# A two-block transformer in exact-split fp32: the weight ring goes from two slots of 2048 columns to four of 1024, and VectorE takes over GpSimd's half of one subtraction

## The reference

```
# first block
u = moba_attention(rms_norm(x), w_qkv, w_o)      # 8 heads of 128; 256 tokens are one block: causal softmax with a distance bias
h = x + rms_norm(u)
h = h + rms_norm(squared_relu_mlp(rms_norm(h)))  # square(relu(h @ w_up)) @ w_down, hidden width 4096
# second block, two layers, each with m = silu(c) @ ada_w + ada_b  (1024 -> 6 * 1024)
x = x + g_m * (mixer(modulate(rms_norm(x), sh_m, sc_m)) @ w_out)
x = x + g_f * swiglu(modulate(rms_norm(x), sh_f, sc_f))   # (silu(h @ w_gate) * (h @ w_up)) @ w_down, hidden width 2816
# mixer of layer 0: w_in (1024 -> 2560), short convolution and a gated linear recurrence (LRU)
# mixer of layer 1: w_qkv, norms of q and k, stick-breaking attention with 16 heads of 64
```

## Time and profile before

| what | value |
|---|---|
| three runs | 1019.25, 1021.16, 1027.04 us; median 1021.16 |
| span of the profiled execution, first to last instruction | 1019.1 us (the profile has no other time of it) |
| mean granted TensorE clock, share of full speed | 0.981 |
| weights and modulation weights read | 206.91 MB from HBM, 204 GB/s over the span |

### The profile page before, as it was taken

How to read it: one execution, slowest core, us unless ns; L and a number is a source line. 1 busy time by engine, 2 the same in 40 slices (tenths; PEclk the granted TensorE clock), 3 DMA queues, 4 the chain that set the end, 5 groups by cost and what they waited for, 6 DMA issues and landing times.

```text
span 1019.1 us, 14930 instructions
## 1 busy us (share of the span) xinstructions
PE 935.0 (92%) x5777; PEld 817.1 (80%) x5777; DVE 693.5 (68%) x582; ACT 447.7 (44%) x481; POOL 527.6 (52%) x224
## 2 busy tenths in 40 slices
PE   5989988999998999779999999989889899999997
PEld 4978777888887688758888898867658698988986
DVE  4378489999999679995678787475997643222234
ACT  4434543334434546535333433365666344333431
POOL 5744454454554365645655555534543445555553
PEclk9999989999999999999999999999889999999999
DMA  6546367888887287552788887434322334554552
GB/s 221 175 134 227 96 251 256 292 319 319 317 312 278 76 312 246 187 205 87 275 305 284 293 305 266 165 124 166 123 83 84 123 125 166 185 185 165 172 192 90
DMA packets 116962, 208.59 MB, mean 205 GB/s; under 512 B 7107, under 2 KB 82987, under 8 KB 110774
## 3 DMA queue, kind: packets, MB, share of 16 engines
q1 hardware_dynamic: 115574, 199.54, 56.1%
q10 hardware_dynamic: 1152, 8.39, 2.3%
q0 software_dynamic: 192, 0.05, 0.0%
HBM read 206.91 MB, written 1.05 MB: 204 GB/s over the span
## 4 chain that ended last, share of the span: by engine, by line
PE 30%; issue 21%; DVE 21%; POOL 18%; ACT 6%; DMA 2%; POOLq 1%; SPq 0%; DVEq 0%; ACTq 0%
POOL w_lo L525 17%; DVE mod L1067 6%; DVE w_lo L940 5%; ACT w_hi L646 4%; PE acc L1397 4%; PE acc L1398 4%; PE acc L1399 4%; PE acc L1452 2%; PE acc L1457 2%; PE acc L1454 2%; DVE x L1021 1%; PE ub L1397 1%; PE ub L1399 1%; PE ub L1398 1%; PE acc L1419 1%
## 5 line engine op out<-in xcount | busy, mean ns | idle before, releaser
L525 POOL TENSOR_TENSOR w_lo<-w_raw,w_hi 128x1024 fp32r<-128x1024 f32 x144 | 464.7, 3227 | 408.0 <-ACT w_hi L646 407.9
L646 ACT ACTIVATE w_hi<-w_raw 128x2048 fp32r<-128x2048 f32 (+1 forms) x144 | 274.4, 1906 | 310.2 <-PE ub L1399 111.4
L940 DVE TENSOR_TENSOR w_lo<-w_raw,w_hi 128x1024 fp32r<-128x1024 f32 x144 | 233.6, 1622 | 167.3 <-ACT w_hi L646 167.0
L1397 PE MATMUL ub<-aT_hi,w_hi 128*128 128x256 f32 x896 | 256.0, 286 | 15.2 <-POOL w_lo L525 10.2
L1398 PE MATMUL ub<-aT_lo,w_hi 128*128 128x256 f32 x896 | 253.6, 283 | 0.0
L1399 PE MATMUL ub<-aT_hi,w_lo 128*128 128x256 f32 x896 | 253.5, 283 | 0.0
L1397 PEld LDWEIGHTS ub<-aT_hi,w_hi 128*128 128x128 f32 x896 | 171.8, 192 | 25.7 <-issue 21.9
L1398 PEld LDWEIGHTS ub<-aT_lo,w_hi 128*128 128x128 f32 x896 | 172.0, 192 | 0.0
L1399 PEld LDWEIGHTS ub<-aT_hi,w_lo 128*128 128x128 f32 x896 | 171.9, 192 | 0.0
L1067 DVE SCALAR_TENSOR_TENSOR mod<-ada_raw,silu_c,mod 128x2048 f32<-128x2048 f32 x46 | 171.8, 3736 | 0.1
L1452 PE MATMUL acc<-w_hi,hT_hi 128*128 128x512 f32 x304 | 123.4, 406 | 6.7 <-issue 3.0
(11 more groups left out here) (229 smaller groups left out, 1198.4 us busy)
## 6 DMA issues: line engine op xcount, KB each, us to landing
ada_raw<-in_l_ada_w SPq DMA_DIRECT2D x40, 1024.0 KB, 7.4
w_raw<-in_l_ffn_w_gate SPq DMA_DIRECT2D x44, 512.0 KB, 4.6
w_raw<-in_l_ffn_w_up SPq DMA_DIRECT2D x44, 512.0 KB, 4.5
w_raw<-in_l_ffn_w_down SPq DMA_DIRECT2D x44, 512.0 KB, 3.9
w_raw<-in_w_up SPq DMA_DIRECT2D x32, 512.0 KB, 4.7
w_raw<-in_w_down SPq DMA_DIRECT2D x32, 512.0 KB, 4.3
w_raw<-in_attn_w_qkv SPq DMA_DIRECT2D x24, 512.0 KB, 4.6
w_raw<-in_l_w_qkv SPq DMA_DIRECT2D x24, 512.0 KB, 4.5
```

Of the source, the lines that this page charges most:

```text
L525: pool.tensor_tensor(w_lo[:, s, LO_V:], w_raw[:, s, LO_V:], w_hi[:, s, LO_V:].bitcast(F32), ALU.subtract).then_inc(lo_p_done, 1)
L646: act.activation(w_hi[:, u % 2, c], w_raw[:, u % 2, c], ACT.Copy).then_inc(hi_done, 1)
L940: dve.tensor_tensor(w_lo[:, s, 0:LO_V], w_raw[:, s, 0:LO_V], w_hi[:, s, 0:LO_V].bitcast(F32), ALU.subtract).then_inc(lo_v_done, 1)
L1397: pe.matmul(outp, ah, bh, start=start and k == 0, stop=False)
```

## The change

The ring keeps its bytes and is cut in four slots of 1024 columns, called parts; a unit is two parts in a row. Each part has its own load semaphore, and `hi_done`, `lo_done` and `w_used` now count parts. The transfers are the same (288 of 512 KB). ScalarE makes `w_hi` with two copies of 1024 columns per unit, VectorE makes both rests of a unit, GpSimd none; GpSimd keeps its other work, with nothing queued between. TensorE waits part by part and multiplies part by part: in `project` and `project_T` the loop over parts is now the outer one, in `down` the loop over the two row blocks, and the last of the three matmuls of a block now follows the other two instead of standing behind all of them. The number of matmuls of each shape stays.

```diff
-LO_V = 1024
+PART = UNIT // 2
+SLOTS = 4
...
-        w_raw = sb("w_raw", [P, 2, UNIT])
+        w_raw = sb("w_raw", [P, SLOTS, PART])
...
-            def load_unit(u, pieces, i=None, per=0):
-                if u >= 2:
-                    sp.wait_ge(lo_v_done, plus(u - 1, i, per))
-                    sp.wait_ge(lo_p_done, plus(u - 1, i, per))
-                for dst, src in pieces:
-                    sp.dma_start(dst, src).then_inc(w_loaded[u % 2], 16)
+            def load_part(v, n, src, i, per):
+                if v >= SLOTS:
+                    sp.wait_ge(lo_done, plus(v - SLOTS + 1, i, 2 * per))
+                dst = w_raw[:, v % SLOTS, :].rearrange("p (k n) -> p k n", n=n)
+                sp.dma_start(dst, src).then_inc(w_loaded[v % SLOTS], 16)
...
-            def split_lo(u, i=None, per=0):
-                if u >= U_END:
-                    return
-                pool.wait_ge(hi_done, plus(u + 1, i, per))
...
-                pool.tensor_tensor(w_lo[:, s, LO_V:], w_raw[:, s, LO_V:], w_hi[:, s, LO_V:].bitcast(F32),
-                                   ALU.subtract).then_inc(lo_p_done, 1)
...
-                act.wait_ge(w_loaded[u % 2], plus(32 * (u // 2 + 1), i, 16 * per))
-                if u >= 2:
-                    act.wait_ge(w_used, plus(u - 1, i, per))
-                c = slice(0, LO_V if u == 0 else UNIT)
-                act.activation(w_hi[:, u % 2, c], w_raw[:, u % 2, c], ACT.Copy).then_inc(hi_done, 1)
+                for v in range(2 * u, 2 * u + (1 if u == 0 else 2)):
+                    act.wait_ge(w_loaded[v % SLOTS], plus(16 * (v // SLOTS + 1), i, 16 * 2 * per // SLOTS))
+                    if v >= SLOTS:
+                        act.wait_ge(w_used, plus(v - SLOTS + 1, i, 2 * per))
+                    act.activation(w_hi[:, v % SLOTS, :], w_raw[:, v % SLOTS, :], ACT.Copy).then_inc(hi_done, 1)
...
-                dve.wait_ge(hi_done, plus(u + 1, i, per))
-                s = u % 2
-                dve.tensor_tensor(w_lo[:, s, 0:LO_V], w_raw[:, s, 0:LO_V], w_hi[:, s, 0:LO_V].bitcast(F32),
-                                  ALU.subtract).then_inc(lo_v_done, 1)
+                for v in range(2 * u, 2 * u + 2):
...
+                        dve.wait_ge(hi_done, hi_count(v, i, per))
+                    n = v % SLOTS
+                    dve.tensor_tensor(w_lo[:, n, :], w_raw[:, n, :], w_hi[:, n, :].bitcast(F32),
+                                      ALU.subtract).then_inc(lo_done, 1)
...
-            def unit_ready(u, i=None, per=0):
-                pe.wait_ge(lo_v_done, plus(u + 1, i, per))
-                pe.wait_ge(lo_p_done, plus(u + 1, i, per))
+            def part_ready(v, i=None, per=0):
+                pe.wait_ge(lo_done, plus(v + 1, i, 2 * per))
...
             def project_T(u, h, banks, i=None, per=0):
...
+                for q in range(2):
+                    v = 2 * u + q
+                    part_ready(v, i, per)
+                    for f in range(2):
+                        outp = banks[f][:, h * TOK:(h + 1) * TOK]
+                        for k in range(4):
+                            c, b = slice(k * HALF + f * P, k * HALF + (f + 1) * P), 4 * q + k
+                            wh, wl = w_hi[:, v % SLOTS, c], w_lo[:, v % SLOTS, c]
+                            pe.matmul(outp, wh, aT_hi[:, b, :], start=b == 0, stop=False)
+                            pe.matmul(outp, wh, aT_lo[:, b, :], start=False, stop=False)
+                            last = pe.matmul(outp, wl, aT_hi[:, b, :], start=False, stop=b == KB - 1)
+                    last.then_inc(w_used, 1)
```

More of the change, by code:

```diff
@@ L570, in _ @@
             for step, n in ATT_STEPS:
-                if step == "H" and n < 16:
-                    split_lo(U_QKV1 + n)
-                elif step == "E" and n < 3:
+                if step == "E" and n < 3:
                     start_sums(0, n * UNIT, (n + 1) * UNIT)
[L575 to L584, removed]
+            for _ in range(4):
+                row_rstd()
             pool.wait_ge(xn_done, 12)
@@ L587, in _ @@
             for step, n in LRU_STEPS:
[L588 to L590 removed]
+                if step == "P":
                     pool.wait_ge(lru_u, 2)
@@ new lines, in project_tile @@
+            def project_tile(v, t, k, outp, op_hi, op_lo, start, stop):
+                s, q = v % SLOTS, slice(t * P, (t + 1) * P)
+                for n in range(2):
+                    c = slice(n * CH, (n + 1) * CH)
+                    pe.matmul(outp, op_hi[:, k + n, q], w_hi[:, s, c], start=start and n == 0, stop=False)
+                    pe.matmul(outp, op_hi[:, k + n, q], w_lo[:, s, c], start=False, stop=False)
+                    last = pe.matmul(outp, op_lo[:, k + n, q], w_hi[:, s, c], start=False, stop=stop and n == 1)
+                return last
@@ new lines, in project @@
+                    pe.wait_ge(y_lo, lo_count)
+                    for q in range(2):
+                        for t in range(NT):
+                            for k in range(2 * q, 2 * q + 2):
+                                c = slice((k % 2) * CH, (k % 2 + 1) * CH)
+                                last = pe.matmul(bank(t), op_lo[:, k, t * P:(t + 1) * P], w_hi[:, (2 * u + q) % SLOTS, c],
+                                                 start=False, stop=h != first and k == 3)
+                        last.then_inc(w_used, 1)
@@ new lines, in project @@
+                    return
+                if tile0:
+                    for t in range(NT):
+                        for q in range(2):
+                            if t == 0:
+                                part_ready(2 * u + q, i, per)
+                            last = project_tile(2 * u + q, t, 2 * q, bank(t), op_hi, op_lo, h == first and q == 0,
+                                                h != first and q == 1)
+                            if t == 1:
+                                last.then_inc(w_used, 1)
+                        if t == 0:
+                            last.then_inc(tile0_done, 1)
+                    return
@@ L1422, in project @@
+                for q in range(2):
+                    part_ready(2 * u + q, i, per)
                     for t in range(NT):
-                        for k in range(4):
-                            last = pe.matmul(bank(t), op_lo[:, k, t * P:(t + 1) * P], rhs[k][0], start=False,
-                                             stop=h != first and k == 3)
+                        last = project_tile(2 * u + q, t, 2 * q, bank(t), op_hi, op_lo, h == first and q == 0,
+                                            h != first and q == 1)
@@ new lines, in down_block @@
+            def down_block(v, k, t, n, start, stop, lo=True):
+                s, q, c = v % SLOTS, slice(t * P, (t + 1) * P), slice(n * CH, (n + 1) * CH)
+                outp = acc[:, 2 * t + n, :]
+                pe.matmul(outp, hT_hi[:, k, q], w_hi[:, s, c], start=start, stop=False)
+                last = pe.matmul(outp, hT_hi[:, k, q], w_lo[:, s, c], start=False, stop=False)
+                if lo:
+                    last = pe.matmul(outp, hT_lo[:, k, q], w_hi[:, s, c], start=False, stop=stop)
+                return last
```

248 lines of the change are left out of this document (114 added, 134 removed).

## The result

The changed kernel takes 953.08 us (median of four runs, 952.81 to 953.43) against 1023.51 (four runs, 1019.25 to 1027.04): a ratio of 0.9319, 95% interval 0.929 to 0.9348.

A forecast was written before the change was run, and what follows sets the result against it. TensorE, busy 935.0 of 1019.1 us, was taken as the main bound, with weight-making setting the end over a good quarter of the span. 1019.1 − 27 − 8 − 13 + 3 = 974, plus 2 for the median: 976 us, range 957 to 1001.

The forecast's parts named there:

- GpSimd's hold: VectorE stands still, marked as busy, while GpSimd subtracts: 56 us excess in the rests, 64 us in the sums.
- Rival D: VectorE's long lengths are its own, so it becomes the bound in MLP and LRU: slower, 1052 us; chance 0.04.
- Rival C: Loads become the bound; MLP and first SwiGLU loops keep their periods, losing 6 + 8 us of gain: 990 us; chance 0.06.
- Rival B: Only MLP and SwiGLU loops gain, 16 + 6 us; attention, LRU and stick-breaking stages do not: 999 us; chance 0.14.
- First term: TensorE's waits for weight rests, 33.5 us in 43 waits, go except a fifth, for units behind norms: −27 us.
- Second term: TensorE's restarts around 43 waits for rests, 0.24 us each beyond the wait's length, four fifths saved: −8 us.
- Third term: Chains GpSimd lengthens without naming a rest (`hT_lo`, first `down` unit, residual additions, three more places): −13 us, sure to half.
- costs: The second rest stands ahead of the norms' work at about three stage ends, 1.1 us each: +3 us.

## Why the prediction was right in kind and too small in size

**The mechanism was right.** VectorE's long lengths were GpSimd's hold: the subtractions that nobody uses bring them back, and memsets don't. And where GpSimd makes every second rest again, the waits that come back name VectorE's rest. Rival D is out with it: VectorE needs 18.59 us of a 22.42 us slice. Rival C is out: both loops run without idle time at 0.91 of the transfer engines. Rival B is out for attention and the LRU, which gave 26 us; in the stick-breaking stage its number holds, with 1.5, but what is late there was not shown: with GpSimd's last subtractions on VectorE TensorE's idle time there grew.

**First term, too small.** Waits that name a rest fell from 33.5 to 0.6 us, −32.9 where I let a fifth stay and took −27. The units behind a norm, for which I kept it, no longer wait for a rest. One wait has only changed its name: at the second half of the LRU's output product TensorE waited 1.6 us for GpSimd's rest and now waits 3.1 for the operand `aT_hi`.

**Second term, the step that failed.** "43 x 0.24 = 10 us, of which four fifths: −8 us" stands for all that TensorE's busy time would lose; it lost 22.8. The price of a restart was right: the second SwiGLU with two of the inserted waits grew by 7.1 us, of which 5.2 idle and some 1.5 low clock, which leaves 0.2 for each restart. What it counted was wrong. It has only the waits that name a rest: all named waits went from 78.2 us in 71 to 33.1 in 27, so 44 restarts went and not 34. And the clock was left out altogether: by windows of 1 us TensorE was granted half speed for 37.6 us before and 20.5 after, the idle end of the program not counted. The two traces tell the parts, if from each of the 5777 matmuls to the start of the next the busy time is set against the median of its shape: 11.9 of the 22.8 us lie in matmuls beside a named wait (0.27 for each of 44), 8.6 in matmuls at the low clock (101 before, 53 after), and 2.3 in all the others. Boundaries without an idle entry, like the one at 252.9, can thus be no more than a small part. The low clock was to be seen in the profile before: in the page's mean of 0.981 and in the 0.96 of the LRU stretch.

**Third term and costs.** Idle time that names no rest fell by 45.3 − 32.9 = 12.4 us, against 13 less 3 of costs. (The five items listed add up to 12.3 and not 13.) That the size fits is in part luck, for the time came only in part from the places listed. The wait for `hT_lo` went, and so did the 3.0 us before the first `down` unit. But the waits for a norm's result fell only from 14.1 to 13.3 in sum, with nothing at the second QKV (1.2 and 1.2), while those for the modulation, which the list does not have, fell from 7.5 to 3.0. The residual additions are at 1285 and 692 ns in the mean, as their short twins foretold, `hT_lo` at 1219 in place of 2868. Of the costs one place shows: in the LRU stage unit 12's two rests (392.21 to 394.56) stand on VectorE ahead of the product for which TensorE waits the 3.1 us. ScalarE's 20 us more of busy time show as no wait of their own.

In sum: 32.9 + 12.4 + 22.8 = 68.1. The low end of the range had the three terms whole and 8 us of unnamed idle time, but restarts for 43 waits alone and no clock.

## What to carry to other kernels

When an instruction shows two lengths for one shape, look at what the other engines do at its start before pricing more of it: here work moved onto the engine that looked saturated made that engine less busy. Two remedies for one wait are not added: each freed the loops alone. And price a wait as its length, the restart, and, where the windows show one behind it, the stretch at 1.2 GHz. In these runs every wait of 3 to 6 us behind the first matmuls had one, and of those of 2.0 to 2.3 us some had one and some had none.

## What was not expected of the hardware

The hold goes to whoever starts second, GpSimd included: the 72 subtractions of 128x1024 that nobody uses took 2.40 to 4.55 us, the longest where a modulation sum had begun 0.05 us ahead. A prefix sum of 128 columns on VectorE is held as well (769 against 425 ns). A wait of 2.0 us at one and the same place cost a stretch at half clock in one program and none in another, so waits of that length have no fixed price.
